# A two-layer hybrid backbone on one core: the first projection's chunks, GLA, taps and attention in another order

## The reference

```
h    = rmsnorm(x, norm1_g) * (1 + sc1) + sh1
proj = h @ w_in                       # 1024 -> 7200 columns
gq, gk, gv, gg, glr, cu, dq, dk, dv, gates = split(proj)
gla  = gated linear attention, forward and backward; decays
       log_sigmoid(glr @ w_a2 + b_a) / 16; rmsnorm(o) * silu(gg)
conv = silu(layernorm(depthwise_conv_31(a * sigmoid(gate))))
diff = 4 heads, two softmaxes each, p1 - lam * p2; axial rotary on
       the sample's queries and keys; the sample also sees 128 cached keys
merged = ga*(gla @ wb1) + gb*(conv @ wb2) + gc*(diff @ wb3)
x = x + g1 * (merged @ w_out)
x = x + g2 * SwiGLU(rmsnorm(x, norm2_g) * (1 + sc2) + sh2)
```

## Time and profile before

| | |
|---|---|
| median of three runs | 1647.55 us (1643.38 to 1650.67) |
| profiled execution | 1645.08 us, span 1643.1 us |
| granted TensorE clock, mean | 0.961 of full speed |
| busy share of the span: TensorE, VectorE, ScalarE, GpSimd | 91%, 46%, 35%, 45% |

### The profile page before, as it was taken

How to read it: one execution, slowest core, us unless ns; L and a number is a source line. 1 busy time by engine, 2 the same in 40 slices (tenths; PEclk the granted TensorE clock), 3 DMA queues, 4 the chain that set the end, 5 groups by cost and what they waited for, 6 DMA issues and landing times.

```text
span 1643.1 us, 22476 instructions
## 1 busy us (share of the span) xinstructions
PE 1490.1 (91%) x9085; PEld 1371.3 (83%) x9085; DVE 756.4 (46%) x1048; ACT 577.7 (35%) x763; POOL 746.4 (45%) x292
## 2 busy tenths in 40 slices
PE   5799778989998999999989979789899899999998
PEld 2688778878898799999968768778789879999997
DVE  2349999244474412210041889962445641212002
ACT  2322332344553433333232233223446243333321
POOL 1343474323345355555534445533334535555551
PEclk8899899999999999999989989999999999999999
DMA  8853222322254355553337422232222533343431
GB/s 315 282 196 90 78 73 75 94 74 65 90 180 128 126 175 187 167 200 128 122 105 252 133 78 77 77 90 71 65 77 90 205 103 120 125 128 128 124 122 63
DMA packets 161262, 208.65 MB, mean 127 GB/s; under 512 B 9228, under 2 KB 135176, under 8 KB 161160
## 3 DMA queue, kind: packets, MB, share of 16 engines
q1 hardware_dynamic: 161160, 207.22, 39.2%
HBM read 204.05 MB, written 3.15 MB: 126 GB/s over the span
## 4 chain that ended last, share of the span: by engine, by line
PE 61%; DVE 25%; ACT 5%; DMA 4%; issue 3%; POOL 1%; SPq 0%; DVEq 0%; ACTq 0%; POOLq 0%
PE ps L596 18%; PE ps L598 17%; PE ps L597 17%; DVE conv_acc L1389 9%; PE ps L548 2%; DVE fac L1518 2%; DMA w_raw<-in_w_out_dram 2%; PE ps L563 2%; POOL w_lo L519 1%; DVE attn L1532 1%; DVE t L1353 1%; DVE fac L1495 1%; DVE prefix L1469 1%; ACT w_hi L1056 1%; DVE mx L1621 1%
## 5 line engine op out<-in xcount | busy, mean ns | idle before, releaser
L519 POOL TENSOR_TENSOR w_lo<-w_raw,w_hi 128x1024 fp32r<-128x1024 f32 x288 | 746.2, 2594 | 867.9 <-ACT w_hi L1056 674.9
L596 PE MATMUL ps<-h_hi,w_hi 128*128 128x384 f32 x1600 | 561.1, 351 | 30.4 <-DVE h_lo L1359 18.7
L597 PE MATMUL ps<-h_lo,w_hi 128*128 128x384 f32 x1600 | 543.6, 340 | 0.0
L598 PE MATMUL ps<-h_hi,w_lo 128*128 128x384 f32 x1600 | 543.5, 340 | 0.0
L1056 ACT ACTIVATE w_hi<-w_raw 128x1024 fp32r<-128x1024 f32 x200 | 211.0, 1057 | 494.5 <-PE ps L598 395.2
L596 PEld LDWEIGHTS ps<-h_hi,w_hi 128*128 128x128 f32 x1600 | 307.3, 192 | 61.3 <-issue 29.4
L597 PEld LDWEIGHTS ps<-h_lo,w_hi 128*128 128x128 f32 x1600 | 307.5, 192 | 1.8
L598 PEld LDWEIGHTS ps<-h_hi,w_lo 128*128 128x128 f32 x1600 | 306.7, 192 | 0.0
L1270 ACT ACTIVATE w_hi<-w_raw 128x1024 fp32r<-128x1024 f32 x88 | 93.4, 1061 | 244.7 <-PE ps L598 228.1
L1389 DVE SCALAR_TENSOR_TENSOR conv_acc<-conv_in,cw,conv_acc 128x399 f32<-128x399 f32 x240 | 177.1, 813 | 0.1
L1676 DVE TENSOR_TENSOR sq<-sq,ps 128x768 f32<-128x768 f32 x22 | 21.0, 954 | 273.3 <-PE ps L598 273.3
(11 more groups left out here) (226 smaller groups left out, 1729.3 us busy)
## 6 DMA issues: line engine op xcount, KB each, us to landing
w_raw<-in_w_in_dram SPq DMA_DIRECT2D x112, 512.0 KB, 3.6
w_raw<-in_w_ffn_in_dram SPq DMA_DIRECT2D x88, 512.0 KB, 3.5
mod_late<-in_w_mod_dram SPq DMA_DIRECT2D x64, 512.0 KB, 5.7
w_raw<-in_w_ffn_out_dram SPq DMA_DIRECT2D x44, 512.0 KB, 3.7
mod_early<-in_w_mod_dram SPq DMA_DIRECT2D x32, 512.0 KB, 5.2
w_raw<-in_w_branch_dram SPq DMA_DIRECT2D x24, 512.0 KB, 3.4
w_raw<-in_w_out_dram SPq DMA_DIRECT2D x16, 512.0 KB, 3.4
out_dram<-stage SPq DMA_DIRECT2D x6, 256.0 KB, 2.3
```

Of the source, the lines that this page charges most:

```text
L519: nc.gpsimd.tensor_tensor(m["w_lo"][:, j], m["w_raw"][:, j % RAW], m["w_hi"][:, j].bitcast(F32), ALU.subtract).then_inc(lo_ready.sem, 1)
L596: mm(out, hi[:, at:at + P], rhs[0][:, k, :], start=start, stop=False)
L597: mm(out, hi[:, at:at + P], rhs[1][:, k, :], start=False, stop=False)
L598: ins = mm(out, lo[:, at:at + P], rhs[0][:, k, :], start=False, stop=stop)
```

## The change

The 29 chunks of the projection come in another order: GLA queries, low-rank rows and keys first, the convolution's gate and input next, then GLA values and gates, and the attention's chunks and branch gates as before. Everything that hangs on them is placed anew: the decay products behind piece 4, level -1 behind 7, levels 0 to 6 and the two whole steps behind 10, 12, ... 26, rotary products behind 25 to 31, the outputs of GLA behind 28 to 31, the attention units behind 34, 35, 37, 39, 40, 42, 44, 45, 47, 49, 50, 52, the convolution's mean behind 53 and its variance behind 55. The modulation vectors 3 and 4 move from pieces 0 to 13 to pieces 11 to 14 and 17 to 20, and vectors 2, 3 and 4 use one bank. ScalarE takes over copies from VectorE (low-rank rows, cached keys, states), the bias of the decays (eight passes on PSUM) and a whole-tile silu with two table loads. VectorE's loop over the levels has no taps; 3, 3, 2, 4 and 4 taps stand between rotary and GLA outputs, and the other 108 in the attention: 2 and 9 in a unit over 384 keys, 2 and 3 in a unit over 128, until all are done. The states are one step, `centre` and `conv_norm` come at the end, and the last two chunks share a bank pair.

The diff, cut to its core, with sixteen columns of indentation taken off inside functions:

```diff
-IN_CHUNKS = ([(C_CG, 256), (C_CA, 256), (C_CG + 256, 256), (C_CA + 256, 256), (C_GG, 256), (C_GG + 256, 256),
-              (C_LR, 2 * RANK), (C_GQ, 256), (C_GK, 256), (C_GV, 256), (C_GV + 256, 256),
+IN_CHUNKS = ([(C_GQ, 256), (C_LR, 2 * RANK), (C_GK, 256), (C_CG, 256), (C_CG + 256, 256), (C_CA, 256), (C_CA + 256, 256),
+              (C_GV, 256), (C_GV + 256, 256), (C_GG, 256), (C_GG + 256, 256),
               (C_DQ, 256), (C_DQ + 256, 256), (C_DK, 256), (C_DK + 256, 256), (C_DV, 256), (C_DV + 256, 256)]
              + [(C_GATE + 256 * i, 256) for i in range(12)])
+K_GQ, K_LR, K_GK, K_CG, K_CA, K_GV, K_GG, K_DQ, K_DV, K_GATE = 0, 1, 2, 3, 5, 7, 9, 11, 15, 17
...
+PAIR_OF = [c % 2 for c in range(27)] + [0, 0]
+MEAN_AFTER, VAR_AFTER = 53, 55
...
+SCORE_AT = [34 + 5 * (u // 3) + (0, 1, 3)[u % 3] for u in range(12)]
+SCORES = {p: u for u, p in enumerate(SCORE_AT)}
+SCORES.update({54: 12, 56: 13})
+HEAD_SUM_AT = (42, 47, 52)
+LEVEL_AT = [10 + 2 * i for i in range(9)]
...
-            return {0: 4, 1: 5, 2: 4, 3: 7, 4: 5, 5: 7}[vec]
+            return {0: 4, 1: 5, 2: 7, 3: 7, 4: 7, 5: 7}[vec]
...
-    if 4 <= s <= 16:
-        if s == 4:
-            sp.wait_ge(*x_ready.at(l, KD))
-            sp.wait_ge(masks_v.sem, 1)
-        for i in ((0, 1, 2) if s == 4 else (3, 4) if s == 5 else (s - 1,)):
-            mod_early(early_at[l, 3, 0] + i)
-    if s == 2:
+    early = {4: (0,), 5: (1,), 6: (2,), 7: (3,), 8: (4,), 15: (5, 6), 16: (7, 8), 17: (9, 10), 18: (11, 12),
+             21: (13, 14), 22: (15,)}
+    if s == 4:
+        sp.wait_ge(*x_ready.at(l, KD))
+        sp.wait_ge(masks_v.sem, 1)
+    for i in early.get(s, ()):
+        mod_early(early_at[l, 3, 0] + i)
+    if s == 0:
...
+        pe.wait_ge(*za.at(l, 4))
+        pe.wait_ge(*evacuated(l, K_GQ))
+        pe.wait_ge(*evacuated(l, K_GK))
...
-    if s <= 6:
-        for k in ((0, 1) if s == 0 else (s + 1,)):
-            mod_mm(l, 3, k)
-    if 7 <= s <= 13:
-        for k in ((0, 1) if s == 7 else (s - 6,)):
-            mod_mm(l, 4, k)
-    if s == 8:
-        mod_turn(l, 2)
-    if s == 10:
-        mod_turn(l, 3)
-    if s == 15:
-        mod_turn(l, 4)
...
+    if s in (9, 16, 21):
+        mod_turn(l, {9: 2, 16: 3, 21: 4}[s])
+    for vec, first in ((3, 11), (4, 17)):
+        if first <= s < first + 4:
+            if s == first:
+                pe.wait_ge(mod_out.sem, vec_at[l, vec])
+            mod_mm(l, vec, 2 * (s - first))
+            mod_mm(l, vec, 2 * (s - first) + 1)
+    if s == 4:
+        pe.wait_ge(*evacuated(l, K_LR))
+        pe.wait_ge(*wa_in.at(l, 32))
+        for i in range(4):
+            for tt in range(NT):
+                ins = mm(ps[:, 4 + tt, P * i:P * i + P], m["wa"][:, i // 2, P * (i % 2):P * (i % 2) + P],
+                         m["lrT"][:, tt * P:tt * P + P], start=True, stop=True)
+        ins.then_inc(z_done.sem, 1)
+    if s == 7:
+        level(-1)
+    if s in LEVEL_AT[:LEVELS]:
+        level(LEVEL_AT.index(s))
+    if s in LEVEL_AT[LEVELS:]:
+        whole(LEVEL_AT.index(s) - LEVELS)
+    if s == 23:
         pe.wait_ge(*ctx_in.at(l, 64))
+        pe.wait_ge(mod_out.sem, vec_at[l, 4] + 1)
         for hh in range(H):
-            ins = nc.tensor.transpose(ps[:, 6, P * hh:P * hh + P], m["ck_rows"][:, P * hh:P * hh + P],
+            ins = nc.tensor.transpose(ps[:, 7, P * hh:P * hh + P], m["ck_rows"][:, P * hh:P * hh + P],
...
-    if s == 17:
...
-        pe.wait_ge(*pair_read[0].at(l, 4))
-        pe.wait_ge(*wa_in.at(l, 32))
-        pe.wait_ge(*small_v.at(l, 3))
-        pe.wait_ge(mod_out.sem, vec_at[l, 4] + 1)
-        for i in range(4):
-            ins = mm(ps[:, 4 + i, 0:T], m["wa"][:, i // 2, P * (i % 2):P * (i % 2) + P], m["lrT"][:],
-                     start=True, stop=True)
-        ins.then_inc(z_done.sem, 1)
-    if s == 19:
-        level(-1)
-    if s in range(21, 21 + 2 * LEVELS, 2):
-        level((s - 21) // 2)
-    if s in (35, 37):
-        whole((s - 35) // 2)
-    if s in (28, 30, 32, 34):
-        rotate((s - 28) // 2)
-    if s == 36:
+    if s in (25, 27, 29, 31):
+        rotate((s - 25) // 2)
+    if s == 33:
         prompt_keys()
-    if s in (38, 40):
-        state((s - 38) // 2)
-    if 39 <= s < 43:
-        gla_out(s - 39)
-    if 40 <= s < 44:
-        head_square_sum(s - 40)
-    if s == 43:
+    if s == 35:
+        state()
+    if 28 <= s < 32:
+        gla_out(s - 28)
+    if 29 <= s < 33:
+        head_square_sum(s - 29)
+    if s == MEAN_AFTER:
         conv_mean()
-    if s == 45:
+    if s == VAR_AFTER:
         conv_var()
-    if s in (50, 53, 56):
-        head_square_sum(H + (s - 50) // 3)
-    if 46 <= s:
-        values(s - 46)
-    if 45 <= s < 57:
-        weights_T(s - 45)
-    if 44 <= s < 56:
-        scores(s - 44)
+    if s in HEAD_SUM_AT:
+        head_square_sum(H + HEAD_SUM_AT.index(s))
+    if s in SCORES:
+        u = SCORES[s]
+        if u >= 2:
+            values(u - 2)
+        if 1 <= u <= 12:
+            weights_T(u - 1)
+        if u < 12:
+            scores(u)
...
+    done = pair_read[PAIR_OF[c]].sem
+    if c == K_GQ:
+        fn(m["gqk"][:, 0, :, :], src, ACT.Copy, scale=DK ** -0.5).then_inc(done, 1)
+    elif c == K_LR:
+        act.wait_ge(*h_lo_ready.at(l, 2 * KD))
+        fn(m["lrT"][:], src[0:2 * RANK, 0, :], ACT.Copy).then_inc(done, 1)
+    elif c == K_GK:
+        fn(m["gqk"][:, 1, :, :], src, ACT.Copy).then_inc(done, 1)
...
+    if s == 8:
+        f0 = m["fac0"][:].rearrange("p a b c d -> p (a b c d)")
+        act.wait_ge(*z_done.at(l, 1))
+        for i in range(4):
+            fn(m["fac0"][:, i // 2, i % 2, :, :], ps[:, 4:7, P * i:P * i + P], ACT.Abs,
+               bias=m["prm"][:, R_BA + i:R_BA + i + 1]).then_inc(za.sem, 1)
+        for i in range(4):
+            fn(m["fac1"][:, i // 2, i % 2, :, :], ps[:, 4:7, P * i:P * i + P], ACT.Identity,
+               bias=m["prm"][:, R_BA + i:R_BA + i + 1]).then_inc(zb.sem, 1)
+        act.wait_ge(*za.at(l, 4))
+        fn(f0, f0, ACT.Exp, scale=-1.0).then_inc(za.sem, 1)
+        act.wait_ge(*za.at(l, 5))
+        fn(f0, f0, ACT.Ln, bias=m["one"][:]).then_inc(za.sem, 1)
+    if s == 13:
         act.preload_act_table_set(LN_EXP)
-        act.wait_ge(*setup_v.at(l, 2))
-        fn(m["lam2"][:, 2:4], m["lam2"][:, 0:2], ACT.Exp).then_inc(setup_a.sem, 1)
...
-    if s == 23:
         act.wait_ge(*scan.at(l, 12))
         for d in range(2):
             fn(m["etot"][:, 2 * d:2 * d + 2], m["prefix"][:, d, :, 1 + d, P], ACT.Exp, scale=1.0 / 16
                ).then_inc(etot_a.sem, 1)
         exp_level(0)
-    if s == 24:
+    if s == 14:
         exp_level(1)
-    if s in range(26, 22 + 2 * ROUNDS, 2):
-        exp_level((s - 22) // 2)
-    if s == 40:
+    if s in range(16, 16 + 2 * (ROUNDS - 2), 2):
+        exp_level((s - 12) // 2)
+    if s == 20:
+        act.wait_ge(*setup_v.at(l, 2))
+        fn(m["lam2"][:, 2:4], m["lam2"][:, 0:2], ACT.Exp).then_inc(setup_a.sem, 1)
+    if s == 27:
+        act.wait_ge(*keys_t.at(l, 1))
+        fn(m["ckT"][:], ps[:, 7, :].rearrange("p (a b) -> p a b", a=H), ACT.Copy).then_inc(keys_a.sem, 1)
+    if s == 31:
+        act.preload_act_table_set("silu_and_others")
+        act.wait_ge(*evacuated(l, K_GG))
+        act.wait_ge(*evacuated(l, K_GG + 1))
+        fn(m["gg"][:], m["gg"][:], ACT.Silu).then_inc(gg_silu.sem, 1)
+        act.preload_act_table_set(LN_EXP)
...
+    if s == 39:
+        act.wait_ge(*st_mm.at(l, 1))
+        if l:
+            act.wait_ge(*st_out.at(l - 1, 32))
+        fn(m["state_out"][:], ps[:, 7, :], ACT.Copy).then_inc(st_a.sem, 1)
+    if 33 <= s < 37:
+        head_rstd_at = s - 34
+        if head_rstd_at >= 0:
+            head_rstd(head_rstd_at)
+        head_squares(s - 33)
+    if s == 37:
+        head_rstd(3)
+    if s == 41:
...
-for i in range(2):
-    dve.wait_ge(*piece_used.at(l, 4 * i + 4))
...
+def conv_gate(i):
...
+    dve.wait_ge(*piece_used.at(l, 2 * (K_CA + i) + 2))
+    dve.wait_ge(*evacuated(l, K_CG + i))
...
-mod_take(l, 2)
-taps(8)
-mod_put(l, 2)
-mod_take(l, 3)
...
-for i in range(2):
-    dve.wait_ge(*gg_sig.at(l, i + 1))
-    g = m["gg"][:, 2 * i:2 * i + 2, :]
-    done(v.tensor_tensor(g, g, pair[i], ALU.mult), pair_read[i], 3)
-    if i == 1:
-        mod_put(l, 3)
-    taps(12)
-dve.wait_ge(*piece_used.at(l, 14))
-done(v.tensor_copy(m["lrT"][:], pair[0][0:2 * RANK, 0, :]), pair_read[0], 4)
-mod_take(l, 4)
-taps(12)
...
-mod_put(l, 4)
-dve.wait_ge(*keys_t.at(l, 1))
-done(v.tensor_copy(m["ckT"][:], ps[:, 6, :].rearrange("p (a b) -> p a b", a=H)), small_v)
-dve.wait_ge(mod_out.sem, vec_at[l, 4] + 1)
-mod_final(16, 40)
-mod_gain(1)
-taps(12)
...
 build(0)
+mod_take(l, 2)
 build(1)
 copy_level(-1)
 multiply(0)
+mod_put(l, 2)
 multiply(1)
 for i in range(2, ROUNDS):
     build(i)
-    taps(10)
+    if i == 2:
+        conv_gate(0)
+    if i == 3:
+        conv_gate(1)
+        lambda_sums()
+    if i == 4:
+        mod_take(l, 3)
+    if i == 5:
+        mod_put(l, 3)
+    if i == 6:
```

(57 more changed lines are left out.)

237 lines of the change are left out of this document (110 added, 127 removed).

## The result

The changed kernel takes 1709.92 us (median of four runs, 1705.60 to 1710.48) where the kernel before takes 1648.24: ratio 1.0372, 95% interval 1.0343 to 1.0402. The forecast was 1637, its range 1609 to 1666.

A forecast was written before the change was run, and what follows sets the result against it. TensorE's time was taken to bound the kernel: per layer 339 us work, 52 waits and 8 slow clock made 399, 5 less than before; 1645.1 - 10.5 + 2.5 gave 1637, range 1609 to 1666.

The forecast's parts named there:

- the forecast's ledger: First projection stage, per layer: 339 us TensorE work, 52 waits, 8 slow clock, 399 in all; before 339, 48, 17.
- 8 us of slow clock in place of 17: Projection stage, per layer: four long waits where TensorE sets the pace, three in GLA and the mean, cost 8 us.
- Item 4: GLA outputs: TensorE waits 3.7, 5 and 4.2 us for ScalarE's norm, VectorE's products, a rotary step and taps; together 12.9.
- Items 1 and 3: Decay products wait 5.9 us for low-rank rows; shared modulation bank, cached keys and second whole-chunk step wait 7.8 together.
- Item 2: First level factors, behind piece 9: ScalarE and VectorE chain of 6.8 us against 4.5, so a wait of 2.3.
- I price both layers alike: Projection stage: the same gain, 5 us less per layer, was taken for both layers, 10 in all.
- Item 5: Attention: VectorE needs 89.2 us plus 21.6 for 18 low halves, 110.8 against TensorE's 95, so TensorE waits 15.8.
- I take 1.2 each: Attention: each of GpSimd's 18 low halves takes 1.2 us from VectorE, 21.6 in all.
- the rival with every low half stopping the taps: Attention: each low half gets in and costs VectorE 2.2 us; this case decides from 1.7 a low half on; chance 0.25.
- the rule of the Trainium skill: Shared VectorE and GpSimd port pair: whoever issues first holds it one instruction, so each low half stops the taps.
- What the change removes: Levels: all waits for factors and rotary sums go, VectorE needing 7.6 us per level; early modulation weights' wait goes too.
- The slower rival at 1673: Attention: 36 low halves cost 1.0 us more each, ending at 1673; its sign was taps of 1 us; chance 0.25.

The follow-up runs named there:

- e8_fill: Changed kernel with unused matmuls issued on TensorE just ahead of its three waits among the GLA outputs, sample output altered: 1694.15 us, ratio 1.0272.
- e1_gla: Changed kernel with ScalarE's squares and inverse roots of the GLA outputs one turn earlier and the fourth rotary step behind the second head's products: 1661.67 us.
- e10: Changed kernel with VectorE's modulation copies ahead of build and the low-rank rows copied one ScalarE turn earlier: 1668.46 us, ratio 1.0133.
- e9: Changed kernel with both GLA output edits, modulation copies ahead of build and low-rank rows copied one ScalarE turn earlier, taps unmoved: 1620.90 us.
- c1: Kernel before the change with GpSimd making only half the columns of each low half after the first four pieces, other half old values: 1574.54 us.

## Why the prediction was wrong

The second layer came out 32 us above the forecast's ledger: +23 slow clock, +15 waits, -6 own work. The first layer came out 12 above the second.

- **The step that failed most is the last one, "8 us of slow clock in place of 17".** I counted four long waits at 2 us each, a price taken from one piece behind one wait. Both factors were low: the profile has nine waits of 3.4 us or more and 30.9 us of slow clock, 3.4 each. Of these, 11.8 stand in the GLA outputs, where three waits of 4 to 6 us leave some 4 each, 10.0 in the attention and 9.2 ahead of both. e8_fill shows the price apart from the waits: 10.6 among the GLA outputs. The kernel before would have shown it: its stretch has seven waits of 2.8 us or more, not eight, and 18.8 us of slow clock, not 17, which is 2.7 each.
- **Item 4, the GLA outputs, was right in place and nearly in size:** waits of 3.7, 5 and 4.2 were forecast, 4.1, 6.4 and 4.7 came. With their clock they are 26 us a layer and 48 in all (e1_gla).
- **Items 1 and 3, decay products and shared bank, were right in place:** 5.9 and 7.8 were forecast; in the second layer 3.5 at the decay products, 9.2 at the bank and the cached keys (L582, L573, L914) and 0.9 at the second whole-chunk step came. Item 2 was 2.3, and 2.4 came. In the first layer the bank cost 14.5, 10.2 of it at the modulation's rows. The step "I price both layers alike" failed by 12 us: 8 are waits and slow clock, 4 own work that the first layer has more of in the kernel before, too (340.5 and 336.9). Bank and decay products are worth 41 in all (e10).
- **Item 5, the attention: "I take 1.2 each" failed.** From the second unit's reduction (1146.5) to the last tap (1273.5) are 127.0 us, in 2.4 of which VectorE waited for scores. Without low halves the count was 89.2, so 18 of them took 35.4, 2.0 each; 17 of the 18 stopped an instruction. That is near the 2.2 of the rival with every low half stopping the taps, and beyond its point of 1.7. TensorE waited 24.3 for VectorE there in place of 15.8. The stretch from which I had 1.2 was of another kind: of its two low halves one stood still through a run of taps and the other ran under three masked copies. In the changed kernel a low half takes 2.47 us on average (2.80 before), so here it comes in behind the tap in flight. That is the rule of the Trainium skill ("SBUF — State Buffer", Who interferes with whom) as the prediction read it against the forecast.
- **Waits that were not on the list** make 5.4: three units' weights wait for ScalarE's inverse roots (3.4), and modulation products for their weights (2.0).
- **What the change removes was right:** levels two pieces apart, no wait for factors over 2.4 us. With the GLA outputs, the bank and the row copy put right (e9), the order gains 27 us.
- **The slower rival at 1673 had a right mechanism and was too low,** since it kept the forecast's 8 us of slow clock. Its sign, taps of 1 us in the attention, came nearly true: 0.94. But c1 shows that its mechanism costs the old order about as much, so the difference between the two kernels isn't there: it is 89 us at three places that the forecast had on its list (items 1, 3 and 4), against a gain of 27. The forecast had charged these places 26.6 us of waits and 6 of slow clock a layer, some 65 in all.
